# Order of the norms' work and of ScalarE's table loads, and what stands ahead of the recurrence's border

## The reference, cut to what matters

```python
for l in range(DEPTH):                                   # DEPTH = 2
    x = x + 0.5 * rms_norm(swiglu(rms_norm(x, ln_ffn1_pre[l]), w_ffn1_in[l], w_ffn1_out[l]), ln_ffn1_post[l])
    mix = token_mixing(rms_norm(x, ln_mix_pre[l]), ...)  # window attention, mLSTM, RWKV-7
    x = x + rms_norm(mix, ln_mix_post[l])
    x = x + 0.5 * rms_norm(swiglu(rms_norm(x, ln_ffn2_pre[l]), w_ffn2_in[l], w_ffn2_out[l]), ln_ffn2_post[l])
    gate = jax.nn.sigmoid(rms_norm(x, ln_ple_pre[l]) @ w_ple_gate[l])
    x = x + rms_norm(gate * (p[l] @ w_ple_proj[l]), ln_ple_post[l])
x = second_block(x, ...)                                 # two attentions and a convolutional FFN
```

## Time and profile before

| | us |
|---|---|
| median of 3 runs | 2913.27 |
| lowest, highest | 2912.16, 2914.24 |
| the profiled execution | 2914.65 |
| its span, first to last instruction | 2912.9 |
| PE busy | 2849.4 (98%) |
| PE weight loads busy | 2402.7 (82%) |
| DVE busy | 1380.4 (47%) |
| ACT busy | 1139.1 (39%) |

### The profile page before, as it was taken

How to read it: one execution, slowest core, us unless ns; L and a number is a source line. 1 busy time by engine, 2 the same in 40 slices (tenths; PEclk the granted TensorE clock), 3 DMA queues, 4 the chain that set the end, 5 groups by cost and what they waited for, 6 DMA issues and landing times. The chain is left out here.

```text
span 2912.9 us, 41085 instructions
## 1 busy us (share of the span) xinstructions
PE 2849.4 (98%) x17248; PEld 2402.7 (82%) x17248; DVE 1380.4 (47%) x1923; ACT 1139.1 (39%) x1635; POOL 15.7 (1%) x29
## 2 busy tenths in 40 slices
PE   7999999999999999999999999999999999999998
PEld 7888888778888888888888877888888889888887
DVE  3333355676333355333336667333346268755641
ACT  3223244545222245222234545332236357534430
POOL 0000000000000000000000000000000000000000
PEclk9999999999999999999999999999999999999999
DMA  4223412103223431223412103122432111222231
GB/s 146 100 94 127 146 35 66 42 3 116 80 95 103 143 122 46 94 94 102 157 51 71 58 8 110 57 96 95 137 123 95 51 56 33 102 73 94 99 126 51
DMA packets 71558, 254.48 MB, mean 87 GB/s; under 512 B 8072, under 2 KB 9224, under 8 KB 71376
## 3 DMA queue, kind: packets, MB, share of 16 engines
q1 hardware_dynamic: 71376, 251.86, 25.8%
HBM read 249.73 MB, written 2.10 MB: 86 GB/s over the span
## 5 line engine op out<-in xcount | busy, mean ns | idle before, releaser
L214 PE MATMUL ps<-h_hi,w_space 128*128 128x512 f32 (+1 forms) x5056 | 1445.4, 369 | 3.4 <-DVE h_lo L312 3.4
L214 PEld LDWEIGHTS ps<-h_hi,w_space 128*128 128x128 f32 x5056 | 919.4, 189 | 164.1 <-DVE h_lo L312 4.2
L202 DVE TENSOR_TENSOR w_space<-w_raw,w_space 128x1024 fp32r<-128x1024 f32 x440 | 533.5, 1224 | 1014.2 <-ACT w_space L195 1014.1
L214 PE MATMUL ps<-h_lo,w_space 128*128 128x512 f32 (+1 forms) x2528 | 930.3, 368 | 0.0
L195 ACT CAST w_space<-w_raw 128x1024 fp32r<-128x1024 f32 x440 | 455.5, 1047 | 898.1 <-PE ps L214 551.0
L224 PE MATMUL ps<-w_space 128*128 128x512 f32 x3216 | 737.3, 390 | 1.3 <-PEq L91 0.8
L224 PEld LDWEIGHTS ps<-w_space 128*128 128x128 f32 x3216 | 601.8, 188 | 126.1 <-issue 1.2
L214 PEld LDWEIGHTS ps<-h_lo,w_space 128*128 128x128 f32 x2528 | 478.0, 189 | 77.9 <-issue 0.5
L589 ACT CAST w_space<-act_p 128x512 fp32r<-128x512 f32 x88 | 54.7, 621 | 186.2 <-DVE act_p L601 186.2
L604 DVE TENSOR_TENSOR w_space<-act_p,w_space 128x512 fp32r<-128x512 f32 x88 | 60.9, 692 | 60.5 <-ACT w_space L589 60.5
L601 DVE TENSOR_TENSOR act_p<-act_s,ps 128x512 f32<-128x512 f32 x88 | 59.9, 681 | 54.9 <-PE ps L214 54.9
(11 more groups left out here) (415 smaller groups left out, 2191.8 us busy)
## 6 DMA issues: line engine op xcount, KB each, us to landing
w_raw<-in_w_ffn_in SPq DMA_DIRECT2D x176, 512.0 KB, 3.4
w_raw<-in_w_ffn_out SPq DMA_DIRECT2D x88, 512.0 KB, 3.5
w_raw<-in_w_in SPq DMA_DIRECT2D x64, 512.0 KB, 3.5
w_raw<-in_w_up SPq DMA_DIRECT2D x44, 512.0 KB, 3.4
w_raw<-in_w_out SPq DMA_DIRECT2D x24, 512.0 KB, 4.0
w_raw<-in_w_down SPq DMA_DIRECT2D x22, 512.0 KB, 3.5
w_raw<-in_w_ple_gate SPq DMA_DIRECT2D x16, 512.0 KB, 3.5
gain_pre<-in_gains_pre SPq DMA_DIRECT2D x10, 512.0 KB, 4.9
```

The lines of the kernel that those rows point to most:

```text
L202: nc.vector.tensor_tensor(self.lo(n), self.raw[:, n % SLOTS, :], self.hi(n).bitcast(F32), ALU.subtract).then_inc(self.lo_ready, 1)
L214: m = nc.tensor.matmul(c.ps[:, bank, t], part[:, cols], moving[:, k, t], start=(k == 0 and i == 0), stop=(k == KD - 1 and i == 2))
```

## The change

**A helper `table`** runs an activation of one column on a constant, into a cell that nothing reads. It makes the load of a function's set fall where the helper stands. It is called with Sqrt at the very front, with Sqrt right behind every sigmoid of the gate stages, and in the recurrence with Exp behind the steps of the state and with Sqrt behind the squares, for t = 1, 2, 3.

**The front's order**: both engines take the norms of tiles 0 and 1 first, then high and low parts of the tiles 0 and 1 with weight units 0 and 1, then tile 2 and unit 2, tile 3 and unit 3.

**The gate stages' order**: the weight units of the next stage are split two at a time, with tiles 1 and 2 ahead of the multiplication, and the last two at the end, where two after tile 0 and four after tile 2 stood.

**The border**: the transposes of the first step's factors and of half of the mLSTM values run ahead of the barrier, `tensor_end` of the factors now holding them around the attention's; `masks` (once) and `g_up` are loaded in the dense stage into fixed places; `select` alone is loaded behind the border. Behind it PE takes the other half of the values, then the gate's product, then the pairs. ACT's `select_r` stands behind the copies of values and gate; DVE's low part of the maximum no longer waits for it.

```diff
+def table(nc, c, function):
+    nc.scalar.activation(c.unread[:, c.tables:c.tables + 1], c.eps[:, 0:1], function)
+    c.tables += 1
...
     def scalar(self, act, nc):
+        turn, W = self.turn, self.c.W
         act.wait_ge(self.c.made, 4)
-        for n in range(NT):
-            self.turn.scalar_pre(act, nc, n)
-            if n:
-                self.turn.scalar_hi(act, nc, n - 1)
-            self.c.W.hi_to(act, nc, n + 1)
-        self.turn.scalar_hi(act, nc, NT - 1)
-        self.c.W.hi_to(act, nc, EARLY)
+        table(nc, self.c, ACT.Sqrt)
+        turn.scalar_pre(act, nc, 0)
+        turn.scalar_pre(act, nc, 1)
+        for n in range(2):
+            turn.scalar_hi(act, nc, n)
+            W.hi_to(act, nc, n + 1)
+        for n in range(2, NT):
+            turn.scalar_pre(act, nc, n)
+            W.hi_to(act, nc, n + 1)
+        for n in range(2, NT):
+            turn.scalar_hi(act, nc, n)
+        W.hi_to(act, nc, EARLY)
...
             nc.scalar.activation(c.s_wide, pair(c, self.gate_bank(n)),
                                  ACT.Sigmoid).then_inc(c.sigmoid, 1)
+            table(nc, c, ACT.Sqrt)
             if n:
                 self.turn.scalar_hi(act, nc, n - 1)
+            if 0 < n < NT - 1:
+                c.W.hi_to(act, nc, self.end() + 2 * n)
             act.wait_ge(c.gated, self.l0 + n + 1)
             self.turn.scalar_post(act, nc, n, c.p_wide)
             self.turn.scalar_pre(act, nc, n)
-            if n == 0:
-                c.W.hi_to(act, nc, self.end() + 2)
-            if n == 2:
-                c.W.hi_to(act, nc, self.end() + EARLY)
         self.turn.scalar_hi(act, nc, NT - 1)
+        c.W.hi_to(act, nc, self.end() + EARLY)
...
             if n:
                 self.turn.vector_lo(dve, nc, n - 1)
+            if 0 < n < NT - 1:
+                c.W.lo_to(dve, nc, self.end() + 2 * n)
             dve.wait_ge(c.sigmoid, self.l0 + n + 1)
...
         sp.dma_start(self.reset[:, :], self.reset_src).then_inc(self.up_loaded, 16)
+        if self.l == 0:
+            sp.dma_start(self.c.rec_masks[:, :, :], self.chunk_masks).then_inc(self.c.rec_loaded, 16)
+        sp.dma_start(self.c.rec_g_up[:, :], self.g_src).then_inc(self.c.rec_loaded, 16)
+
+    def tensor_end(self, pe, nc):
+        c, mix, attention = self.c, self.mix, self.attention
+        pe.wait_ge(self.factors, 4)
+        pe.wait_ge(self.scaled, 4)
+        pe.wait_ge(attention.rough_read, HEADS)
+        pe.wait_ge(self.bonus_ready, 2)
+        turn_factors(nc, c, mix, 0)
+        self.proj.wait_tile(pe, MV_T + 1)
+        attention.tensor_end(pe, nc)
+        turn_values(nc, c, 0)
...
-                sp.dma_start(g_up[:, :], loras[l, 1]).then_inc(loaded, 16)
-                sp.dma_start(masks[:, :, :], chunk_masks).then_inc(loaded, 16)
                 sp.dma_start(select[:, :, :], selectors).then_inc(loaded, 16)
...
-                turn(0)
-                values_by_token()
-                pairs_of_a(0)
-                pe.wait_ge(loaded, 48)
+                turn_values(nc, c, 1).then_inc(v_turned, 1)
+                pe.wait_ge(c.rec_loaded, 16 * (l + 2))
                 for j in range(2):
                     nc.tensor.matmul(c.ps[:, j, :], g_up[:, j * P:(j + 1) * P], mix[:, G_AT, :], start=True,
                                      stop=True).then_inc(gate_done, 1)
+                pairs_of_a(0)
...
                     if t:
                         steps_of_state(t - 1)
+                        table(nc, c, ACT.Exp)
                     powers(t, 2)
...
                     if t:
                         squares(t - 1)
+                        table(nc, c, ACT.Sqrt)
                     solution(t)
...
-                dve.wait_ge(loaded, 48)
-                dve.wait_ge(run_first, 2)
+                dve.wait_ge(c.rec_loaded, 16 * (l + 2))
+                dve.wait_ge(run_first, 1)
```

More of the change, by code:

```diff
@@ L1485, with turn_factors, turn_values @@
 STEPS = 5
+ROW_BANKS, SCORE_BANK, SUM_BANK = (2, 3), 5, 7
+def turn_factors(nc, c, mix, t):
+    cols = slice(t * P, (t + 1) * P)
+    for q, src in enumerate((c.proj[:, FA:FA + 2, :], c.proj[:, FB:FB + 2, :], mix[:, K_AT:K_AT + 2, :], mix[:, V_AT:V_AT + 2, :])):
+        for j in range(2):
+            at = (2 * (q % 2) + j) * P
+            m = nc.tensor.transpose(c.ps[:, ROW_BANKS[q // 2], at:at + P], src[:, j, cols], c.mat["ident"])
+    return m
+def turn_values(nc, c, i):
+    for n in range(2):
+        for j in range(2):
+            m = nc.tensor.transpose(c.ps[:, (SCORE_BANK, SUM_BANK)[i], (2 * n + j) * P:(2 * n + j + 1) * P],
+                                    c.proj[:, MV_T + j, (2 * i + n) * P:(2 * i + n + 1) * P], c.mat["ident"])
+    return m
 def recurrence_stage(nc, c, l, selectors, loras, chunk_masks, mixout):
@@ L1569, in turn @@
                 def turn(t):
-                    cols = slice(t * P, (t + 1) * P)
                     if t == 1:
                         pe.wait_ge(masked, 2)
-                    elif t:
+                    else:
                         pe.wait_ge(gh_copied, 2 * (t - 1))
-                    for q, src in enumerate((f_a, f_b, f_k, None)):
-                        for j in range(2):
-                            at = (2 * (q % 2) + j) * P
-                            m = nc.tensor.transpose(c.ps[:, ROW_BANKS[q // 2], at:at + P],
-                                                    src[:, j, cols] if src is not None else mix[:, V_AT + j, cols],
-                                                    c.mat["ident"])
-                    m.then_inc(turned, 1)
+                    turn_factors(nc, c, mix, t).then_inc(turned, 1)
                 def corners(t, left, right, at):
@@ L1929, in _ @@
                 nc.scalar.copy(run_hi, run_max).then_inc(run_first, 1)
-                act.wait_ge(loaded, 48)
-                nc.scalar.copy(select_r[:, :, :], select[:, :, :]).then_inc(run_first, 1)
                 for i in range(2):
-                    act.wait_ge(v_turned, i + 1)
+                    if i:
+                        act.wait_ge(v_turned, i)
                     nc.scalar.copy(v_tok[:, 2 * i:2 * i + 2, :, 0:DH],
@@ L1938, in _ @@
                     nc.scalar.copy(gate[:, j, :], c.ps[:, j, :]).then_inc(gate_ready, 1)
+                act.wait_ge(loaded, 16)
+                nc.scalar.copy(select_r[:, :, :], select[:, :, :]).then_inc(run_first, 1)
                 act.wait_ge(u_turned, 1)
```

56 lines of the change are left out of this document (29 added, 27 removed).

## The result

| | us |
| --- | --- |
| changed kernel, median of 5 runs | 2927.38 (2923.0 to 2931.99) |
| kernel before, median of 5 runs beside them | 2912.98 (2912.14 to 2914.24) |
| ratio, 95% interval | 1.0047 (1.0036 to 1.0058) |
| the profiled execution of the changed kernel | 2925.99, span 2924.2, mean granted clock 0.993 |

The time was forecast at 2906.7, at most 2910.5; it is 14.4 above the kernel before. The front, the borders and the third step of the recurrence gained what the prediction said of them or more; if the start of the same matmul is compared in the two traces ("by position", from here on), the changed kernel is 7.3 us ahead at 645 us. All of that and 11 us more is lost in two kinds of places that each occur twice: the end of a recurrence (about 4.7 each, 4.3 of it at half clock) and a gate stage (about 7.2 each, all of it and more at the third token tile).

The account below looks back on a forecast made before the run. PE was taken as the bound, working 2849 of 2913 us, so only its idle time or clock could be won. Terms -2.3 - 5.6 - 0.5 + 1.8 = -6.6 gave 2906.7 us from the median; range 2903.5 to 2910.5.

Parts of the forecast that it names:

- The front: Program start: earlier Sqrt load brings tokens sooner, PE's first product near 16.9; -2.3 us, bounds -1.7 and -3.1.
- the borders: Two borders ahead of the recurrences: transposes and loads moved ahead shorten the path to `a_values`; -2.5 and -3.1 us.
- the third step of the recurrence: Recurrence at t = 2: the Exp load leaves the path and PE's wait of 1.33 goes; -0.88 us.
- The failed step: Gate stage, tile 2: two splits ahead of the multiplication make the norm 2.5 us later, still 0.3 before PE wants it.
- the sum: Whole kernel: -2.3 front, -5.6 borders, -0.5 recurrence, +1.8 gate stages, together -6.6 us, giving 2906.7; chance 0.55.
- My bounds for the two stages together: Both gate stages: +3.5 us if tile 2's slack of 0.3 is used up, -2 if the high part comes in time.
- The gate stage's loads: Gate stages: Sqrt load behind the sigmoid delays the high part; PE's gate product of tile 3 comes 1.05 us later.
- The term of -5.6: Both borders together: shorter path from first transpose to `a_values`; -5.6 us, bounds -4.0 and -6.5.
- clock at the border stays low: Rival at the borders: half clock remains, so they give -4.0 to -4.5 us; about 2908; chance 0.22.
- The recurrence: Recurrence steps: Exp load leaves the path, each Sqrt load costs `local` 0.45 us at t = 1, 2, 3; -0.23 a layer.
- The term of -0.5: Recurrences of both layers: net effect of the moved Exp and Sqrt loads, -0.5 us; bounds 0 to -2.6.
- the slower rival: Rival in the recurrence: moved pauses lower the granted clock in more 4.00 us stretches; 2913 to 2919 us; chance 0.04.

Follow-up runs that it names:

- r6: Kernel before plus the changed front, borders and the recurrence's Exp loads, without Sqrt loads there, gate stages as before: 2902.83 us, ratio 0.9969.
- r5: Kernel before plus only the gate stages' new order of weight splits, no table loads added: 2922.30 us, ratio 1.0033.
- r1: Changed kernel with the gate stages' weight splits back in their old places, Sqrt loads kept: 2915.80 us, ratio 1.0013.
- r2: Changed kernel without the Sqrt loads behind the gate stages' sigmoids, new split order kept: 2923.02 us, ratio 1.0041.
- r10: New front, borders and Exp loads; gate stages without table loads, first split pair ahead of tile 1's multiplication, the rest as before: 2902.18 us, ratio 0.9959.
- r11: New front, borders and Exp loads, plus the Sqrt load behind each gate-stage sigmoid, weight splits in the old order: 2908.89 us, ratio 0.9986.
- r9: Kernel before plus only the changed borders: 2910.24 us, ratio 0.9988.
- r8: Kernel before plus only the changed front (early Sqrt load, order of first splits): 2910.58 us, ratio 0.9992.
- r4: Changed kernel with gate stages as before and both recurrence loads removed, leaving only front and borders changed: 2908.36 us, ratio 0.9985.
- r3: Changed kernel with the gate stages wholly as before; front, borders and both recurrence loads kept: 2909.59 us, ratio 0.9991.
- r7: Kernel before plus the changed front, borders and the recurrence's Sqrt loads, without Exp loads, gate stages as before: 2909.79 us, ratio 0.9988.

## Why the prediction was wrong, step by step

**The failed step** is one sentence on the gate stage: "Behind it DVE splits two units ahead of the multiplication (2 x 1.15), which makes tile 2's norm 2.5 later, still 0.3 before PE wants it." It prices the splits by their own length on DVE. But a split is a cast on ACT first, and the cast has a wait of its own: it writes a slot that the gate product of tile 3 still reads, and the slots are released only by the last token tile. So the pair costs not 2.3 but, from the end of `h_lo` at 1118.8 to the multiplication at 1126.86, 8.1; in r6 the multiplication stands 0.5 behind `h_lo`. PE's wait for `h_tokens` went from nothing to 5.22 in the first stage and 5.57 in the second, and the clock fell during it. By position the first stage wins 0.6 at tile 1's gate product, loses 1.5 at tile 3's, 5.4 in this wait and 2.0 by the lower clock, and wins 1.2 back at the last turn: 7.2 net, where the sum had 0.9; the second stage likewise. r5 shows it alone (+9.1), r1 and r2 take the two parts apart, r10 shows that the same kind of move with free slots is harmless. I had looked at what stands behind the moved work and not at what the moved work itself waits for. My bounds for the two stages together, +3.5 to -2, were drawn around lengths, and didn't hold it.

**The gate stage's loads**: the mechanism was right and the size too small. The forecast was a new wait of about 1.4 ahead of tile 3's gate product; it is 1.19, and the product came 1.5 later by position for the 1.05 of the sum. In the change the delay at tile 1's gate product is made up by the first pair of casts, whose move wins 1.1 to 1.2 there (r5, r10); without it, in r11, that wait grows from 0.86 to 2.35, and the loads cost 2.9 a stage. The sum had 0.9.

**The front**: the path was right. `h_tokens` of tile 0 at 7.12 (7.01 forecast), of tile 1 at 10.91 (11.28), the first product at 16.58 (16.9) for the 19.18 of the earlier trace rows:

```profile
5.34 1.06 ACT L272 ACTIVATE junk<-x 128x1024 bf16<-128x1024 f32 x1 [3.10 <-DMA x<-in_x]
...
15.30 1.22 DVE L312 TENSOR_TENSOR h_lo<-ps,h_hi 128x1024 fp32r<-128x1024 f32 x1 [0.84 <-ACT h_hi L280]
...
16.58 0.58 PE L214 MATMUL ps<-h_hi,w_space 128*128 128x256 f32 x1 [2.36 <-DVE h_lo L312]
```

The trace is 3.7 ahead from 26 us on, because the pace of PE's first products also rose at 19.9 us where it rose at 25.0. That part isn't the change's: between kernels with the same front the rise moves by some 3 us, from 19.5 to 23.0 in the eleven traces with the new front, from 22.2 to 25.0 in the three with the old one (before, r5, r9), and r5 and r9 are already 1.1 and 0.7 ahead of before with an unchanged front. Taken by group, the median of the lead is 3.2 with the new front and 0.7 with the old, a difference of 2.4, and r8 has 2.6 by its runs, against -2.3 in the sum.

**The borders**: the path was right. From the first transpose behind the border (561.14) to `a_values` (565.49) it takes 4.35 for a forecast of 4.2, where the earlier trace rows has 6.94; at the second border it takes 4.35 as well (1683.01 to 1687.36), where the earlier trace rows gives 7.64. The last head's transposes aren't late:

```profile
558.23 0.93 PE L1530 MATMUL ps<-mats,proj 128*128 128x128 f32 x7
...
559.25 0.63 PE L1120 MATMUL ps<-mats,dense_start_o_tok 128*128 128x128 f32 x4
...
561.14 0.63 PE L1538 MATMUL ps<-mats,proj 128*128 128x128 f32 x4 [0.82 <-PEq L91]
561.61 1.88 PE L1828 MATMUL ps<-proj,rec_g_up 128*128 128x512 f32 x4
...
565.49 0.68 PE L1654 MATMUL ps<-rec_tok,rec_pair_t 64*64 64x64 f32 x16 [1.14 <-DVE rec_pair_t L2037]
```

By position the change gains 2.6 at each border (the second has half clock just behind `a_values`, which costs 0.7), for a forecast of 2.5 and 3.1: the size held too. The term of -5.6 came out at -2.7 in r9 by the medians (-5.8 at its interval's end). Of the missing part, 1.5 is the stretch of half clock that then appears in the first recurrence's third step. The rival "clock at the border stays low" was also right in part: of the eleven traces with the new border seven are at half clock at the first, near 568 (there the gain is 1.2 to 1.4), and four at the second; the profiled execution of the change is so at the second only.

**The recurrence**: right on the waits. The wait of 1.33 is gone, the one at t = 3 shrank from 1.38 to at most 1.1, and PE's sum for the weighted scores went from 7.2 to 4.0. Each Sqrt load moved PE's `local` by 0.3 for the 0.45 of the sum. By position a layer gains 0.7 up to there, for the 0.23 of the sum. The term of -0.5 was wrong in both directions: the Exp load is worth far more (r6 is 6.9 further below before than r4), because the clock of the products behind the wait of 1.3 often fell too, as the earlier trace rows showed for 1738 us. I had read that row as a risk and not as part of the price of the wait ahead of it. And the Sqrt load beside it brings the slower rival's case, which I gave 0.04: the clock falls at the recurrence's end. Its mechanism held, its place and size didn't: two stretches of 10.2 us instead of four more of 4.00, worth about 4.3 each. Where both come they eat 8.6 of the gain. The measured time lies beyond the rival's 2913 to 2919 all the same, because the gate stages' loss isn't in it.

The load itself is as the prediction had it: 1.28, with the one-column activation 1.30 behind its start (1115.09 and 1116.39). The drain of 1380 ns of the Trainium skill's page "ScalarE: Activation LUTs", section "What ACT_TABLE_LOAD costs", is in none of the rows shown here.

**Where the 21 us between forecast and result are.** The steps from r3 (-2.3) by way of r1 (+3.9) to the change (+14.4) give the gate stages 16.7 where the sum had 1.8: 14.9 (by position the two stages lose 14.3). The rest of the change came to -2.3 (r3) where the sum had -8.4: 6.1. Together 21.0. These are differences of medians that each carry an uncertainty of about 3 us.

## What to carry to other kernels

When work is moved ahead in an engine's queue, ask first what the moved work itself waits for (here a buffer whose reader was still running), and only then how long it takes. A short wait of PE among small matmuls can cost more than its own length, by the slower products behind it; look at the granted clock right after each wait before pricing it. A change of many parts is worth running in parts: one that was 0.5% slower as a whole held a gain of 0.3 to 0.4%.

## What the chip showed that I hadn't expected

The granted clock decided more than the instructions did. A wait of 1.3 us at t = 2 was followed, in six of twelve cases, by half clock that cost 1.5 us; during a wait of 5.2 in the gate stage the clock fell for 6.9 us, which cost 2.0 more; and between executions of the same kernel (r3) the mean granted clock varied from 0.994 to 0.998, for 2905.75 to 2915.00 us. Two edits that each left the clock alone (r6, r7: in 16 of 18 executions 0.998 or more) lowered it together (r3: 0.998 in three of ten). So gains of single edits needn't add up here: on front and borders (r4, -3.5) the Exp loads give -10.4 and the Sqrt loads -3.4, and both together -2.3. Front and borders themselves, -2.6 and -2.7 alone and -3.5 together, agree within the noise.
